# Standing weights stored in alternate words, second activation views moved by 96 bytes

## The chip, the cores and the metric

The kernel runs on one core of one Trainium2 chip, in one launch. The metric is device time in microseconds. Three runs of the kernel before took 1596.76 us in the median (1593.56 to 1600.59).

## The reference, cut to what matters

Two transformer blocks are computed for 256 tokens of width 2048, all in float32. Nearly all of the work is in products of a 256-row activation with a large weight matrix:

```
def first_block(x, c, ...):
    mod = silu(c) @ w_ada + b_ada                  # 2048 x 6144, one row
    h = rms(x) * (1 + scale) + shift
    proj = h @ w_in                                # 2048 x 8192
    ...                                            # chunked attention, gated recurrence
    return x + gate * (concat([att, hg]) @ w_out)  # 2048 x 2048

def second_block(x, mem, ...):
    z = rms(x) @ w_in_2                            # 2048 x 1856
    ...                                            # pooling, latent attention, attention to mem @ w_mem_kv
    x = x + concat([y_pool, y_mla, y_mem]) @ w_o
    h = rms(x)
    return x + (silu(conv3(h @ w_gate)) * (h @ w_up)) @ w_down   # w_gate, w_up: 2048 x 5632
```

## The kernel before

**Products in three parts.** TensorE multiplies in its fast float32 form, which keeps fewer digits. So every weight and every activation stands in SBUF as a high part and a low part, and a product is high times high, high times low activation, and low weight times high activation. Weights come by DMA into the ring `raw` (1 MB each, two halves of 1024 words in each partition). For each half h, ScalarE copies it to the high part (line 1519) and VectorE subtracts to get the low part (line 1916). They go to two tiles, `wh` and `wl`, of four slots each (`WS`), slot h % 4, 4096 bytes a slot. TensorE waits for a half's low part, uses it, and frees the slot with a semaphore.

**Two kinds of halves.** In a *standing* half (function `s`, lines 1169 to 1174) each 128 x 128 block of weights is loaded into the array, and the activations are streamed past it. A block has three matmuls of 256 columns, lines 1169 (high weights, high activations), 1170 (high weights, low activations) and 1171 (low weights, high activations); in the gate and up products of the last stage, the first two are one matmul of 512 columns (line 1173), and the third is line 1174. Every matmul has its own weight load. There are 2736 standing blocks in 342 halves: 512 for `w_in` (reading the view `hA`), 240 for `w_in_2` (`hA2`), 576 for `w_out`, `w_o` and the up-projections (`hB2`), and 1408 for gate and up (`hA2`, the wide ones). In a *moving* half (functions `m`, `chunk`, `memory_row`, `down_part`) it is the other way round: activations are loaded into the array, and 512 columns of weights are streamed. These are lines 1309 to 1311, 1216 to 1218, 1192 to 1194 and 1226 to 1228.

**Where things lie.** In each partition `wh` begins at byte 49280, `wl` at 65664, `hA` at 82048, `hB` at 133248: all at 128 past a multiple of 512. An activation tile of `hA` or `hB` is 2048 bytes: 256 high words, then 256 low words. `hA2` and `hB2` are second views over the same space, 32 bytes further on, used by later stages. A weight block is 512 bytes. The blocks, the parts of an activation and the tiles of each view thus all keep one distance to each other modulo 512: 0 for `hA` and `hB`, 32 for the second views. In the built program the weight load of a block walks its columns from the last to the first (step -1), and the activations are streamed from the first to the last.

**The order of the work** is written by a planner (class `Order`), which keeps TensorE's stream of halves full and puts the small work of attention, recurrence and norms between blocks in six lanes. It plans with its own table of costs, which the change does not touch.

Of the kernel before, what the change touches and what calls it, by code (L numbers as in the profile page):

```python
# [7 lines left out]
F32 = mybir.dt.float32  # L8
# [6 lines left out]
P = 128  # L15
# [11 lines left out]
LANES = 6  # L27

# [187 lines left out]
class Order:  # L216
# [3 lines left out]
    def __init__(self):  # L220
# [32 lines left out]
        self.second = set()  # L253
        self.events = []
# [210 lines left out]
    def m_half(self, tile, banks, kts, buf, first, last):  # L465
        h = self.half
        self.half += 1
        self.want(h + self.ahead)
        self.half_start(h)
        self.beat("m", h, banks, buf, kts, first, last, tile, [self.seen(buf, kt) for kt in kts])  # L470
# [12 lines left out]
    def chunk_half(self, g, n, kt, pair):  # L483
        h = self.half
        self.half += 1
        self.want(h + self.ahead)
        self.half_start(h)
        kts = GROUPS[g][1]
        self.beat("c", h, g, kt, pair, self.seen("A", kt))
        if kt == kts[-1]:  # L490
            for c in (2 * pair, 2 * pair + 1):
                self.beat("part", h, g, c)

    def memory_row(self, kt):
        h = self.half
        self.half += 1
        self.want(h + self.ahead)
        self.half_start(h)
        self.beat("mm", h, kt)

    def down_half(self, kt, pair):
# [3 lines left out]
        self.half_start(h)  # L505
        self.beat("down", h, kt, pair, self.seen("F", kt))
# [3 lines left out]
    def down_end(self, kts):  # L510
# [3 lines left out]
        self.half_start(self.half - 1)  # L514
        self.beat("dend", h, kts)
# [339 lines left out]
def program(nc, table, wts, ada, xN, xT, memN, crow, cst, vec, msk, wpool, dt, out):  # L855
    o = order()
    with ExitStack() as ctx:
# [10 lines left out]
        wh = sb("wh", [P, WS, HALF], F32R)  # L868
        wl = sb("wl", [P, WS, HALF], F32R)
# [3 lines left out]
        at[0] += 32  # L873
# [5 lines left out]
        early = nc.alloc_sbuf_tensor_at("early", [P, 4096], F32, offset=at[0] + 32)  # L879
        E1 = nc.alloc_sbuf_tensor_at("E1", [P, 512], F32, offset=at[0] + 32 + 15 * 2048)[:, :]  # L880
        hB_off = at[0]
        hB = sb("hB", [P, KT, 512], F32R)
        at[0] += 32
# [40 lines left out]
        mark, after = counts.mark, counts.after  # L924

# [188 lines left out]
        def _(e):  # L1114
# [23 lines left out]
            for b in o.beats:  # L1138
                if b[0] == "load" and b[1] >= RAW:
                    load(b[1])  # L1140
                elif b[0] == "consts":
                    e.dma_start(mk[:].rearrange("p a b -> p (a b)"), msk).then_inc(s_mask, 16)
# [12 lines left out]
        def _(e):  # L1155
            def s(h, j, bank, buf, kt, first, last, tile, fresh):
                hl = moving[buf][:, kt % KT, :]
                w1, w2 = wh[:, h % WS, j * P:(j + 1) * P], wl[:, h % WS, j * P:(j + 1) * P]
# [21 lines left out]
            def m(h, banks, buf, kts, first, last, tile, fresh):  # L1180
                e.wait_ge(s_lo, h + 1)
                for j, kt in enumerate(kts):
                    w1, w2 = wh[:, h % WS, j * 512:(j + 1) * 512], wl[:, h % WS, j * 512:(j + 1) * 512]
# [13 lines left out]
            def chunk(h, g, kt, pair, fresh):  # L1197
# [4 lines left out]
                for i in (1, 0) if g == 0 and kt == kts[0] and pair == 0 else (0, 1):  # L1202
                    c = 2 * pair + i
                    w1, w2 = wh[:, h % WS, i * 512:(i + 1) * 512], wl[:, h % WS, i * 512:(i + 1) * 512]
# [16 lines left out]
            def down_part(h, kt, c, t, first, last):  # L1221
                w1, w2 = (w[:, h % WS, c % 2 * 512:c % 2 * 512 + 512] for w in (wh, wl))
# [75 lines left out]
            def memory_row(h, kt):  # L1298
                e.wait_ge(s_lo, h + 1)
                e.wait_ge(*moving_ready("B", kt))  # L1300
                for i in (1, 0) if kt == 0 else (0, 1):
                    if kt == 0 and i == 0:
                        e.wait_ge(*after(("open",), "dve", ("cb", 3)))
                    w1, w2 = wh[:, h % WS, i * 512:(i + 1) * 512], wl[:, h % WS, i * 512:(i + 1) * 512]
# [209 lines left out]
        def _(e):  # L1514
            def split(h, n, part):
# [3 lines left out]
                e.activation(wh[:, h % WS, :], raw[:, n % RAW, part * HALF:(part + 1) * HALF], ACT.Copy).then_inc(s_hi)  # L1519
# [392 lines left out]
        def _(e):  # L1912
            def split(h, n, part):
                src = raw[:, n % RAW, part * HALF:(part + 1) * HALF]
                e.wait_ge(s_hi, h + 1)
                e.tensor_tensor(wl[:, h % WS, :], src, wh[:, h % WS, :].bitcast(F32), ALU.subtract).then_inc(s_lo)  # L1916
# [111 lines left out]
            def rec(t, k):  # L2028
# [3 lines left out]
                def pick(li):  # L2032
# [8 lines left out]
                    if li == 0:  # L2041
                        src = bank[:, :].rearrange("p (a w) -> p a w", a=4)
                        mask = mk[:, 0, :].unsqueeze(1).broadcast_to([P, 4, P])
                    else:
# [4 lines left out]
                        mask = mk[:, li, 0:64].rearrange("p (n w) -> p n w", w=h).unsqueeze(1).broadcast_to([P, 4, n, h])  # L2049
# [481 lines left out]
def constants():  # L2531
# [30 lines left out]
    return c, m.reshape(P, -1)  # L2562
# [65 lines left out]
```

## Time and profile before

| | |
|---|---|
| median of the runs | 1596.76 us |
| the profiled execution, span | 1599.0 us |
| PE busy, matmuls | 1573.0 us (98%), 9650 |
| PEld busy, weight loads | 1400.7 us (88%), 9650 |
| DVE busy | 1154.1 us (72%) |
| ACT busy | 862.4 us (54%) |
| chain that ended last | PE 89%, DVE 5%, DMA 3% |

The page comes from one execution. Its share of busy time says that an engine had some instruction in it, not that it worked at its peak: a matmul of 256 columns is shown as 0.28 us long, while the next one starts 0.12 us after it. What a matmul costs in a dense stream is therefore read from the distance of starts. A weight load (PEld) runs beside the matmul before its own. The granted clock is at its higher level, 2.4 GHz, in nearly every slice.

### The profile page before, as it was taken

To read this page: it belongs to the slowest core of one execution; us is meant where nothing else is said; L and a number is where in the kernel's file an instruction comes from. 1 tells how busy PE (TensorE), PEld (TensorE's weight loads), DVE (VectorE), ACT (ScalarE), POOL (GpSimd) and SP (SyncE) were. 2 spreads that over 40 slices of the span, in tenths; PEclk is the share of its full clock that TensorE was granted. 3 is DMA by queue.
4 is the path that set the end of the run, shared out by engine and by line. 5 is a ranking of instruction groups with operands and counts; after the bars stand their busy time and mean duration, and the time that the engine had idled before them with its cause. 6 is when DMAs were issued, how large, how long until landed. Compare 5 with 4: busy or idle time off the path is not lost.

```text
span 1599.0 us, 24289 instructions
## 1 busy us (share of the span) xinstructions
PE 1573.0 (98%) x9650; PEld 1400.7 (88%) x9650; DVE 1154.1 (72%) x1696; ACT 862.4 (54%) x1321; POOL 151.6 (9%) x164
## 2 busy tenths in 40 slices
PE   8998999989999999999999999999999999999999
PEld 6787889988999999988799888888888888888887
DVE  6797867877778886759778777777777777455544
ACT  6855546767665555655556454544444444444442
POOL 0000000321221220034213000000000000000000
PEclk9999999999999999999999999999999999999999
DMA  9999975533457774343244545555455454555552
GB/s 373 369 343 349 365 285 209 188 114 121 180 189 267 285 272 179 132 158 132 97 144 178 189 170 199 184 186 210 172 197 191 179 211 175 205 199 185 198 196 105
DMA packets 47825, 331.02 MB, mean 207 GB/s; under 512 B 5281, under 2 KB 6689, under 8 KB 8417
## 3 DMA queue, kind: packets, MB, share of 16 engines
q1 hardware_dynamic: 45184, 312.20, 53.5%
q0 software_dynamic: 2240, 17.04, 2.8%
q8 instruction: 76, 1.25, 0.3%
q14 instruction: 35, 0.29, 0.1%
q10 hardware_dynamic: 290, 0.25, 0.1%
HBM read 327.37 MB, written 2.10 MB: 206 GB/s over the span
## 4 chain that ended last, share of the span: by engine, by line
PE 89%; DVE 5%; DMA 3%; ACT 2%; issue 1%; POOL 0%; SPq 0%; ACTq 0%; DVEq 0%; POOLq 0%
PE ps L1173 20%; PE ps L1174 11%; PE ps L1169 9%; PE ps L1170 8%; PE ps L1171 8%; PE ps L1228 5%; PE ps L1227 5%; PE ps L1226 5%; PE ps L1216 4%; PE ps L1217 3%; PE ps L1218 3%; DVE wl L1916 2%; DMA raw<-in_wts 1%; DMA xs<-in_xN 1%; PE ps L1384 1%; PE ps L1351 1%
## 5 line engine op out<-in xcount | busy, mean ns | idle before, releaser
L1916 DVE TENSOR_TENSOR wl<-raw,wh 128x1024 fp32r<-128x1024 f32 x512 | 626.2, 1236 | 282.4 <-ACT wh L1519 281.9
L1519 ACT ACTIVATE wh<-raw 128x1024 fp32r<-128x1024 f32 x512 | 531.3, 1054 | 377.2 <-PE ps L1228 130.6
L1173 PE MATMUL ps<-hA,wh 128*128 128x512 f32 x1408 | 488.7, 390 | 0.0
L1174 PE MATMUL ps<-hA,wl 128*128 128x256 f32 x1408 | 397.0, 282 | 0.0
L1173 PEld LDWEIGHTS ps<-hA,wh 128*128 128x128 f32 x1408 | 264.2, 188 | 55.3
L1174 PEld LDWEIGHTS ps<-hA,wl 128*128 128x128 f32 x1408 | 266.1, 189 | 0.0
L1169 PE MATMUL ps<-hA,wh 128*128 128x256 f32 x752 | 219.5, 292 | 0.0
L1170 PE MATMUL ps<-hA,wh 128*128 128x256 f32 x752 | 211.7, 282 | 0.0
L1171 PE MATMUL ps<-hA,wl 128*128 128x256 f32 x752 | 211.7, 282 | 0.0
L1169 PE MATMUL ps<-hB,wh 128*128 128x256 f32 x576 | 164.4, 285 | 0.8 <-DVE work L2362 0.4
L1170 PE MATMUL ps<-hB,wh 128*128 128x256 f32 x576 | 161.1, 280 | 0.0
L1171 PE MATMUL ps<-hB,wl 128*128 128x256 f32 x576 | 160.6, 279 | 0.0
L1169 PEld LDWEIGHTS ps<-hA,wh 128*128 128x128 f32 x752 | 143.2, 190 | 2.7 <-issue 1.9
L1170 PEld LDWEIGHTS ps<-hA,wh 128*128 128x128 f32 x752 | 143.3, 191 | 0.7 <-issue 0.2
L1171 PEld LDWEIGHTS ps<-hA,wl 128*128 128x128 f32 x752 | 143.1, 190 | 0.0
L1226 PE MATMUL ps<-wh,hB 128*128 128x512 f32 x352 | 137.0, 389 | 0.0
L1227 PE MATMUL ps<-wl,hB 128*128 128x512 f32 x352 | 136.9, 389 | 0.0
L1228 PE MATMUL ps<-wh,hB 128*128 128x512 f32 x352 | 136.9, 389 | 0.0
L1169 PEld LDWEIGHTS ps<-hB,wh 128*128 128x128 f32 x576 | 108.2, 188 | 5.2 <-issue 4.0
L1170 PEld LDWEIGHTS ps<-hB,wh 128*128 128x128 f32 x576 | 108.3, 188 | 0.3 <-issue 0.2
L1171 PEld LDWEIGHTS ps<-hB,wl 128*128 128x128 f32 x576 | 108.3, 188 | 0.0
L1216 PE MATMUL ps<-wh,hA 128*128 128x512 f32 x256 | 101.4, 396 | 4.2 <-ACT xs L1701 3.3
(303 smaller groups left out, 2077.9 us busy)
## 6 DMA issues: line engine op xcount, KB each, us to landing
raw<-in_wts SPq DMA_DIRECT2D x256, 1024.0 KB, 4.8
raw<-in_ada SPq DMA_DIRECT2D x36, 1024.0 KB, 6.1
side<-in_ada POOLq DMA_DIRECT2D x12, 1024.0 KB, 8.5
work<-in_memN SPq DMA_DIRECT2D x2, 1024.0 KB, 8.9
xs<-in_xN POOLq DMA_DIRECT2D x1, 2048.0 KB, 20.6
xs<-in_xT POOLq DMA_DIRECT2D x2, 1024.0 KB, 7.8
out_rows<-xs SPq DMA_DIRECT2D x8, 256.0 KB, 2.4
wp<-in_dt SPq DMA_DIRECT2D x8, 128.0 KB, 2.7
```

Of the source, the lines that this page charges most:

```text
L1169: e.matmul(po, w1, hl[:, 0:T], start=first, stop=False)
L1170: e.matmul(po, w1, hl[:, T:2 * T], start=False, stop=False)
L1171: i = e.matmul(po, w2, hl[:, 0:T], start=False, stop=last)
L1173: e.matmul(ps[bank][:, :], w1, hl, start=first, stop=False)
L1174: i = e.matmul(ps[bank][:, T:2 * T], w2, hl[:, 0:T], start=False, stop=last)
L1216: e.matmul(po, hi, w1, start=kt == kts[0], stop=False)
L1217: e.matmul(po, hi, w2, start=False, stop=False)
L1226: e.matmul(po, hi, w1, start=first, stop=False)
L1227: e.matmul(po, hi, w2, start=False, stop=False)
L1228: return e.matmul(po, lo, w1, start=False, stop=last)
L1519: e.activation(wh[:, h % WS, :], raw[:, n % RAW, part * HALF:(part + 1) * HALF], ACT.Copy).then_inc(s_hi)
L1916: e.tensor_tensor(wl[:, h % WS, :], src, wh[:, h % WS, :].bitcast(F32), ALU.subtract).then_inc(s_lo)
```

## The change

The two tiles `wh` and `wl` become one, `wb`, with four slots of 8192 bytes, in the same space. A new function `weights(h)` says where the parts of half h lie. For a moving half they lie as before, 1024 high words and then 1024 low words (`o.moved` holds these halves). For a standing half they lie column by column in alternate words: high in the even words, low in the odd ones. So ScalarE writes every second word of the slot, VectorE reads one set and writes the other, and a weight load of TensorE walks 128 words in steps of two, over 1024 bytes instead of 512. The activations are still streamed forwards.

The second views `hA2` and `hB2` lie 128 bytes past the first ones (`VIEW`) instead of 32. The mask tile `mk` is packed (576 bytes instead of 1024) to make room for that. The instructions of every engine, their order and their waits are the same; only the addresses and steps of operands differ, and the DMA of the masks is smaller.

```
+VIEW = 128
...
-        wh = sb("wh", [P, WS, HALF], F32R)
-        wl = sb("wl", [P, WS, HALF], F32R)
+        wb = sb("wb", [P, WS, 2 * HALF], F32R)
...
         hA = sb("hA", [P, KT, 512], F32R)
-        at[0] += 32
+        at[0] += VIEW
...
-        early = nc.alloc_sbuf_tensor_at("early", [P, 4096], F32, offset=at[0] + 32)
+        early = nc.alloc_sbuf_tensor_at("early", [P, 4096], F32, offset=at[0] + VIEW)
...
-        mk = sb("mk", [P, len(LEVELS), P], U8, 1)
+        mk = sb("mk", [P, P + 64 * (len(LEVELS) - 1)], U8, 1)
...
-        hA2 = nc.alloc_sbuf_tensor_at("hA2", [P, KT, 512], F32R, offset=hA_off + 32)
-        hB2 = nc.alloc_sbuf_tensor_at("hB2", [P, KT, 512], F32R, offset=hB_off + 32)
+        hA2 = nc.alloc_sbuf_tensor_at("hA2", [P, KT, 512], F32R, offset=hA_off + VIEW)
+        hB2 = nc.alloc_sbuf_tensor_at("hB2", [P, KT, 512], F32R, offset=hB_off + VIEW)
...
+        def weights(h):
+
+            slot = wb[:, h % WS, :]
+            if h in o.moved:
+                return slot[:, 0:HALF], slot[:, HALF:2 * HALF]
+            return slot[:, 0::2], slot[:, 1::2]
...
             def s(h, j, bank, buf, kt, first, last, tile, fresh):
                 hl = moving[buf][:, kt % KT, :]
-                w1, w2 = wh[:, h % WS, j * P:(j + 1) * P], wl[:, h % WS, j * P:(j + 1) * P]
+                w1, w2 = (w[:, j * P:(j + 1) * P] for w in weights(h))
...
-                e.activation(wh[:, h % WS, :], raw[:, n % RAW, part * HALF:(part + 1) * HALF], ACT.Copy).then_inc(s_hi)
+                e.activation(weights(h)[0], raw[:, n % RAW, part * HALF:(part + 1) * HALF], ACT.Copy).then_inc(s_hi)
...
                 e.wait_ge(s_hi, h + 1)
-                e.tensor_tensor(wl[:, h % WS, :], src, wh[:, h % WS, :].bitcast(F32), ALU.subtract).then_inc(s_lo)
+                hi, lo = weights(h)
+                e.tensor_tensor(lo, src, hi.bitcast(F32), ALU.subtract).then_inc(s_lo)
```

## Rows read from the trace of the kernel before

**Rows 1.** Stretches by stage: us busy and count of PE, PEld, DVE, ACT, POOL; clock, DMA.

```profile
0.00:251.00 251.00, 238.11 (x1028) 192.47 (x1029) 191.44 (x205) 144.72 (x206) 7.26 (x17) 0.98 0.90 341
251.00:863.00 612.00, 602.48 (x4711) 572.89 (x4711) 473.90 (x817) 382.15 (x664) 142.06 (x145) 0.99 0.49 177
863.00:1356.00 493.00, 493.00 (x2860) 437.54 (x2859) 368.00 (x553) 236.53 (x338) 2.27 (x2) 1.00 0.52 188
1356.00:1599.00 243.00, 239.46 (x1056) 197.78 (x1055) 120.74 (x125) 98.99 (x114) 0.00 (x0) 1.00 0.51 182
```

**Rows 2.** Timeline of PE in the `w_in` product (view `hA`): start us, length, line.

```profile
420.87 0.28 PE L1171 MATMUL ps<-hA,wl 128*128 128x256 f32 x1
...
422.19 0.28 PE L1170 MATMUL ps<-hA,wh 128*128 128x256 f32 x1
```

**Rows 3.** The same in the `w_in_2` product (view `hA2`, 32 bytes on).

```profile
637.05 0.28 PE L1169 MATMUL ps<-hA,wh 128*128 128x256 f32 x1
...
638.22 0.28 PE L1170 MATMUL ps<-hA,wh 128*128 128x256 f32 x1
```

**Rows 4.** The wide line 1173 in 1000 to 1300 us: shortest/median/longest ns, first and last start.

```profile
L1173 PE MATMUL ps<-hA,wh x866: 390/390/390, 999.8 to 1299.7; 128*128 128x512 f32 x174
```

**Rows 5.** Timeline of PE in that stage.

```profile
1101.04 0.39 PE L1173 MATMUL ps<-hA,wh 128*128 128x512 f32 x1
1101.27 0.28 PE L1174 MATMUL ps<-hA,wl 128*128 128x256 f32 x1
1101.38 0.39 PE L1173 MATMUL ps<-hA,wh 128*128 128x512 f32 x1
```

**Rows 6.** Line 1226, moving weights, one of three equal matmuls, 1400 to 1590 us.

```profile
L1226 PE MATMUL ps<-wh,hB x280: 389/389/472, 1400.0 to 1589.9; 128*128 128x512 f32 x140
```

**Rows 7.** The chain of waits: start, us, what. Transposes of 128 columns, each with a load.

```profile
886.92 1.75 PE ps L1263 x16
```

**Rows 8.** Timeline of PE: float32 matmuls in two passes each, 256 columns.

```profile
635.84 0.59 PE L1395 MATMUL ps<-work 128*128 128x256 f32 x2
636.27 0.59 PE L1399 MATMUL ps<-work 128*128 128x256 f32 x2
```

**Rows 9.** VectorE, 256 columns from SBUF: lines 2067 (steps of two and more) and 2308 (dense).

```profile
L2067 DVE TENSOR_TENSOR work<-E,work x6: 407/416/465, 350.5 to 487.5; 128x256 f32<-128x256 f32 x6
L2308 DVE TENSOR_TENSOR work<-ps,work x88: 416/422/426, 870.8 to 1357.1; 128x256 f32<-128x256 f32 x88
```

**Rows 10.** The page's costliest groups: busy us, mean ns, idle before and its releaser.

```profile
L1916 DVE TENSOR_TENSOR wl<-raw,wh 128x1024 fp32r<-128x1024 f32 x512 | 626.2, 1236 | 282.4 <-ACT wh L1519 281.9
L1519 ACT ACTIVATE wh<-raw 128x1024 fp32r<-128x1024 f32 x512 | 531.3, 1054 | 377.2 <-PE ps L1228 130.6
```

**Rows 11.** Stretches of the mixed stages, columns as in Rows 1.

```profile
300.00:350.00 50.00, 45.53 (x338) 43.07 (x337) 38.33 (x85) 32.68 (x64) 14.01 (x14) 0.93 0.36 128
350.00:400.00 50.00, 46.85 (x358) 44.23 (x357) 40.47 (x94) 38.18 (x80) 13.23 (x15) 0.97 0.35 122
...
550.00:575.00 25.00, 24.61 (x205) 23.85 (x204) 24.86 (x31) 10.91 (x17) 4.55 (x4) 1.00 0.88 335
```

**Rows 12.** The chain of waits in the `w_out` product.

```profile
556.67 2.20 DVE raw L1962
558.87 0.02 DVE cols L1962
...
559.04 1.22 DVE wl L1916
560.26 0.39 DVE xs L2348
560.65 1.13 DVE wl L1916
```

More of the change, by code:

```diff
@@ L253, in __init__ @@
         self.second = set()
+        self.moved = set()
         self.events = []
@@ L498, in memory_row @@
         self.half_start(h)
+        self.moved.add(h)
         self.beat("mm", h, kt)
@@ L505, in down_half @@
         self.half_start(h)
+        self.moved.add(h)
         self.beat("down", h, kt, pair, self.seen("F", kt))
@@ L514, in down_end @@
         self.half_start(self.half - 1)
+        self.moved.update(range(h, h + 2 * len(kts)))
         self.beat("dend", h, kts)
@@ L1182, in m @@
                 for j, kt in enumerate(kts):
-                    w1, w2 = wh[:, h % WS, j * 512:(j + 1) * 512], wl[:, h % WS, j * 512:(j + 1) * 512]
+                    w1, w2 = (w[:, j * 512:(j + 1) * 512] for w in weights(h))
                     if fresh[j]:
@@ L1203, in chunk @@
                     c = 2 * pair + i
-                    w1, w2 = wh[:, h % WS, i * 512:(i + 1) * 512], wl[:, h % WS, i * 512:(i + 1) * 512]
+                    w1, w2 = (w[:, i * 512:(i + 1) * 512] for w in weights(h))
                     if kt == kts[0]:
@@ L1221, in down_part @@
             def down_part(h, kt, c, t, first, last):
-                w1, w2 = (w[:, h % WS, c % 2 * 512:c % 2 * 512 + 512] for w in (wh, wl))
+                w1, w2 = (w[:, c % 2 * 512:c % 2 * 512 + 512] for w in weights(h))
                 hi = hB[:, kt % KT, t * P:(t + 1) * P]
@@ L1303, in memory_row @@
                         e.wait_ge(*after(("open",), "dve", ("cb", 3)))
-                    w1, w2 = wh[:, h % WS, i * 512:(i + 1) * 512], wl[:, h % WS, i * 512:(i + 1) * 512]
+                    w1, w2 = (w[:, i * 512:(i + 1) * 512] for w in weights(h))
                     for t in range(2):
@@ L2042, in pick @@
                         src = bank[:, :].rearrange("p (a w) -> p a w", a=4)
-                        mask = mk[:, 0, :].unsqueeze(1).broadcast_to([P, 4, P])
+                        mask = mk[:, 0:P].unsqueeze(1).broadcast_to([P, 4, P])
                     else:
@@ L2048, in pick @@
                         src = bank[:, 0:T].rearrange("p (a n w) -> p a n w", a=4, w=h)
-                        mask = mk[:, li, 0:64].rearrange("p (n w) -> p n w", w=h).unsqueeze(1).broadcast_to([P, 4, n, h])
+                        mask = mk[:, P + 64 * (li - 1):P + 64 * li].rearrange("p (n w) -> p n w", w=h).unsqueeze(1).broadcast_to([P, 4, n, h])
                     e.copy_predicated(dst, mask, src).then_inc(mark(t, "dve", ("p", li)))
@@ L2561, in constants @@
             m[:, n, 0:64] = (s // (2 * h) == late // (2 * h)) & (s % (2 * h) < h)
-    return c, m.reshape(P, -1)
+    return c, np.concatenate([m[:, 0]] + [m[:, n, 0:64] for n in range(1, len(LEVELS))], 1)
 def kernel(**inputs):
```

8 lines of the change are left out of this document (5 added, 3 removed).

## The prediction

> **What bounds the kernel now.** I read the stages first [rows 1]. From 251 to 1356 us, where all standing halves lie, TensorE is busy nearly throughout: 602 of 612 us, then 493 of 493. In the wide stage VectorE has 368 us of work in 493 and ScalarE 237, so both follow TensorE. What a block costs on TensorE is what that stage costs. So the question is how far apart its matmuls start, and why.
>
> In the `w_in` product eleven steps take 422.19 - 420.87 = 1.32 us: 120.0 ns for a matmul of 256 columns [rows 2]. At the granted 2.4 GHz 256 columns are 106.7 ns; 13.3 ns are on top. The same matmuls over the view that lies 32 bytes further take 1.17 us for ten steps, 117 ns [rows 3]. The instructions are alike, the distance of the addresses is not: part of the surcharge hangs on where weights and activations lie to each other. In the wide stage a block takes 299.9 / 865 = 346.7 ns [rows 4], about 230 and 115 [rows 5]; 768 columns are 320, so 26.7 ns are on top, 13.3 for each matmul again. With moving weights it is (189.9 / 279) / 3 = 226.9 ns, against 213.3 for 512 columns [rows 6]: again 13.5.
>
> Two kinds of rows have nearly no surcharge. Sixteen transposes of 128 columns, each with its load, take 1.75 us, 109.4 ns each [rows 7]. A stream of 128 columns would be 53 ns, so this is the load of 128 weight columns: 106.7 ns at one column per cycle of 1.2 GHz, and 2.7. And float32 matmuls of 256 columns in two passes start 0.43 / 2 = 215 ns apart [rows 8]: there a pass takes in one column per cycle of 1.2 GHz (213.3 ns), just as the load beside it, and only some 2 ns are on top. In the fast form the stream takes eight bytes in that time and the load four, and 13 ns are on top.
>
> **The change part by part.** The reading of these rows on which I build: a load and a stream that read SBUF at the same time now and then want the same piece of it, and one of them is held up; how often depends on their distance and on their relative pace. This is inferred, no row shows a held-up read.
>
> *Loads of standing weights in steps of two words.* They now pass eight bytes for each column, as many as the stream does in the same time. The nearest rows with equal pace have 2 to 3 ns on top [rows 7, 8]. That is the good end: 109.4 ns for a matmul of 256 columns (it can't go below the load) and 213.3 + 2.1 + 109.4 = 324.8 for a wide block. The other end is that the load fetches pieces of fixed size, twice as many as before, and each has the same price: 13.3 ns more for each load. I take 112 ns for 256 columns and 331 for a wide block, nearer to the first end, since the equal pace is the property that both cheap rows share; I do not take the end itself, since in them a stream at half rate has time to catch up, and here it has none.
>
> The count: `w_in` has 512 blocks or 1536 matmuls, 1536 x (120 - 112) = 12.3 us. The other narrow ones are 816 blocks or 2448 matmuls, 2448 x (117 - 112) = 12.2 us. The wide ones are 1408 x (346.7 - 331) = 22.1 us. Together 46.6 us of TensorE. At the good end: 1536 x 10.6 + 2448 x 7.6 + 1408 x 21.9 = 16.3 + 18.6 + 30.8 = 65.7 us.
>
> *What of it reaches the end.* The wide stage: all, since VectorE's 368 us and ScalarE's 237 fit into 493 - 22 = 471 [rows 1]. In the `w_in` stage TensorE already waits at 300 to 400 us (busy 92.4 of 100) with the other engines at 71 to 79 us [rows 11]; its recurrence hangs on VectorE, ScalarE and GpSimd. I keep half of the 12.3 us. In the `w_out` product VectorE is busy for 24.86 of 25 us [rows 11], and the chain of waits runs through it alone [rows 12]: conversions, sums and the 2.2 us products for the gate's modulation. There, some 30 us long, a faster TensorE brings nothing, 30 x 4% = 1.3 us; with the attention tails I take 3 us off the 12.2. So 6.1 + 9.2 + 22.1 = 37 us are left.
>
> *The conversions write and read every second word.* There are 342 such halves, 1.24 us each on VectorE and 1.05 on ScalarE [rows 10]. VectorE operations of 256 columns in steps of two and more take 416 ns, dense ones 422 [rows 9]: the step costs nothing, and I take zero. No row shows ScalarE writing in steps. Its bounds are zero and one more such instruction, 1.05 us for each half; over the 176 wide halves that is 185 us on top of 237, still under 471, so the price would be lateness at a half's start, which three halves of lead hide. If VectorE did pay its 1.24 us twice, it would need 368 + 218 = 586 us in that stage and be the bound; [rows 9] speaks against it, and I leave it in the slow cases.
>
> *Moving halves.* High and low part are now 4096 bytes apart, not 16384; modulo 512 nothing changes, and the first views lie as before. I take 0; at 1 ns either way for each of 2040 matmuls it would be 2 us.
>
> *The second views 128 bytes on.* A shift of 32 bytes was worth 3 ns of 120 [rows 2, 3]. With equal pace and both walks in opposite directions the distance decides where they meet, so the shift may be worth anything between the ends above. It is in the 112. The 24 matmuls that load from `hB2` (lines 1192 to 1194) are too few to count. The packed mask saves 57 KB of one DMA that nobody waits for.
>
> **The Trainium skill.** The rows show that the surcharge moves with the address, 120.0 against 117 ns [rows 2, 3]. The Trainium skill, "TensorE: Matmul & The Clock Gate", Part 2, says that TensorE has two independent SBUF read ports, so that loading the next weights takes nothing from the running matmul; by this rule the change would do nothing, the third rival below. The rows speak against the rule's strict form. The Trainium skill, "SBUF — State Buffer", Specifications, says that lines are 16 bytes and that two hits on each are needed for the full rate; steps of two float32 words give just two. No row here has a load in steps; if it failed, that is the second rival.
>
> **The rivals.** (1) *Twice the pieces, twice the stalls*: slower. Each standing load today carries up to 13.3 ns and would carry 13.3 more. There are 3984 narrow and 2816 wide loads: 6800 x 13.3 = 90 us, 1687 us. It decides once a load's surcharge goes above today's 10 to 13 ns. For it: in all dense fast-form rows the surcharge goes with the load, whether the stream has 256 or 512 columns [rows 2, 5, 6], as if each load had a fixed number of pieces. Against it: the same load beside a float32 stream costs 2 ns [rows 8]. (2) *A load in steps of two runs at half rate*: 109.4 x 2 = 219 ns. The narrow matmuls would cost 219 instead of 118, 3984 x 101 = 402 us, and the narrow half of a wide block 219 instead of 115, 146 us: about 2145 us. (3) *The surcharge is not reading but the exchange of weights in the array*: no change, 1597 us. For it: that it is 13.3 in three places; against it: [rows 3, 7]. (4) *Only one kind of view gains*: where the distance is unlucky the stream still meets the load as often as before. With the first views alone, 6 us: 1591; this is hardly to be told from no change.
>
> **How the numbers follow.** Profiled: 1599.0 - 37 = 1562; the median of the runs is 2.2 us lower, so 1560. Chances: the forecast, both kinds of view gaining, 0.55; rival 1 in any size 0.21; rival 2 or a VectorE that pays for steps 0.04; rival 3 0.10; rival 4 0.10, half of which lies beyond 0.5%. About 0.5%, 8 us, is what a measurement can tell from no change. So faster 0.60, same 0.15, slower 0.25. The range runs from the good end, 1597 - 66 = 1531, over no change, to 1612, where a mild form of rival 1 (2 ns for each load) still lies; the strong forms stay outside.
>
> **What would show it.** Right: in the profile of the changed kernel, steps of about 112 ns at lines 1169 to 1171 and 331 ns for a wide block, VectorE's line for the low part still at about 1.24 us, ScalarE's at 1.05. Wrong: steps of 130 ns or more (rival 1), 219 (rival 2), 120 and 347 (rival 3), or second views that stay at 117 and 347 while `hA` falls (rival 4). If TensorE's steps fall and the time does not, look at 300 to 400 and 540 to 575 us for VectorE.

## The result, and the profile after

The changed kernel takes 1620.26 us in the median of four runs (1617.19 to 1621.64). The kernel before, run beside it, takes 1597.72 us (1593.56 to 1600.59). The ratio is 1.0137 (95% interval 1.0117 to 1.0157): 22 us slower. The profiled execution has a span of 1615.4 us against 1599.0.

The first view is the page of the changed kernel: totals, then its costliest groups (line, operation, shapes, count | us busy, mean ns of one | idle before and its releaser).

```profile
PE 1591.8 (99%) x9650; PEld 1418.6 (88%) x9650; DVE 1155.4 (72%) x1696; ACT 894.5 (55%) x1321; POOL 151.2 (9%) x164
...
L1930 DVE TENSOR_TENSOR wb<-raw,wb 128x1024 fp32r<-128x1024 f32 x512 | 626.0, 1236 | 295.3 <-ACT wb L1532 294.5
L1532 ACT ACTIVATE wb<-raw 128x1024 fp32r<-128x1024 f32 x512 | 564.3, 1121 | 373.0 <-PE ps L1241 130.5
L1186 PE MATMUL ps<-hA,wb 128*128 128x512 f32 x1408 | 501.1, 401 | 0.0
L1187 PE MATMUL ps<-hA,wb 128*128 128x256 f32 x1408 | 394.7, 280 | 0.0
L1186 PEld LDWEIGHTS ps<-hA,wb 128*128 128x128 f32 x1408 | 277.8, 197 | 56.5
```

The lines have moved: 1169 to 1171 are now 1182 to 1184, 1173 and 1174 are 1186 and 1187, 1226 is 1239, 1519 is 1532, 1916 is 1930. VectorE's low parts cost what they did, 1236 ns a half [rows 10]. ScalarE's high parts went from 1054 to 1121 ns in the mean. That mean mixes moving and standing halves. If the 67 ns belong to the 342 standing halves of 512, each of these takes 67 x 512 / 342 = 100 ns more. Half by half the trace shows just that: 342 copies went from 1053 to 1152 ns in the mean, the other 170 stayed within 2 ns. Columns here: shortest/median/longest ns, first and last start.

```profile
L1532 ACT ACTIVATE wb<-raw x512: 1039/1140/1215, 11.3 to 1600.9; 128x1024 fp32r<-128x1024 f32 x171
```

Next, stretches by stage, with the columns of [rows 1] (busy us and count of PE, PEld, DVE, ACT, POOL; clock, DMA).

```profile
251.00:863.00 612.00, 603.62 (x4659) 575.11 (x4659) 468.66 (x808) 394.74 (x658) 140.15 (x143) 0.99 0.49 176
863.00:1356.00 493.00, 493.00 (x2799) 438.21 (x2798) 359.78 (x539) 248.03 (x334) 3.81 (x4) 1.00 0.51 184
```

In both kernels TensorE fills the stretch from 863 to 1356 us, at the same clock of 1.00. Before, it got 2860 matmuls in [rows 1]; now it gets 2799. At about 178 ns each, these 61 are 11 us. From 251 to 863 us it is 52 fewer (4711 before), at about 120 ns 6 us. So the loss lies where standing weights are used, and it is a price per matmul: TensorE is never idle longer in the wide stage, it is busy all along and gets less done.

The wide line of the changed kernel, from 1000 to 1300 us, answers to [rows 4], and the timeline of TensorE in that stage (start us, length us, line) to [rows 5]:

```profile
L1186 PE MATMUL ps<-hA,wb x845: 398/401/403, 999.9 to 1300.0; 128*128 128x512 f32 x169
L1186 PEld LDWEIGHTS ps<-hA,wb x844: 197/197/198, 1000.1 to 1299.9; 128*128 128x128 f32 x169
```

```profile
1101.10 0.28 PE L1187 MATMUL ps<-hA,wb 128*128 128x256 f32 x1
1101.22 0.40 PE L1186 MATMUL ps<-hA,wb 128*128 128x512 f32 x1
1101.45 0.28 PE L1187 MATMUL ps<-hA,wb 128*128 128x256 f32 x1
1101.57 0.40 PE L1186 MATMUL ps<-hA,wb 128*128 128x512 f32 x1
```

A wide block takes (1300.0 - 999.9) / 844 = 355.6 ns, against 346.7. It is all in the matmul of 512 columns: in the mean 238.9 ns to the next start instead of 228.3, while the 256 columns behind it take 116.7 instead of 118.3. Over 1408 blocks, 8.9 ns are 12.5 us.

The narrow matmuls over the first view did not change: here the `w_in` product again, sixteen starts of which the first and the last are shown, (422.58 - 420.78) / 15 = 120.0 ns as in [rows 2].

```profile
420.78 0.28 PE L1182 MATMUL ps<-hA,wb 128*128 128x256 f32 x1
...
422.58 0.28 PE L1182 MATMUL ps<-hA,wb 128*128 128x256 f32 x1
```

Those over the second view `hB2` did. First the kernel before, then the changed one, in the same stretch of their `hB2` products; 40 starts lie between the first and last row of the former, 39 in the latter:

```profile
839.76 0.28 PE L1169 MATMUL ps<-hB,wh 128*128 128x256 f32 x1
...
844.59 0.28 PE L1171 MATMUL ps<-hB,wl 128*128 128x256 f32 x1
```

```profile
839.76 0.28 PE L1183 MATMUL ps<-hB,wb 128*128 128x256 f32 x1
...
844.61 0.29 PE L1184 MATMUL ps<-hB,wb 128*128 128x256 f32 x1
```

That is 4.83 / 41 = 117.8 ns before and 4.85 / 40 = 121.2 after. The mean over all narrow matmuls of the second views rose by as much, from 117.1 to 120.7. Over these 2448, 3.5 ns are 8.6 us. With the wide blocks it makes 21 us of the measured 22.

The two profiled executions show where this arrives: the first line of the narrow blocks over `hA` and `hA2`, before and after, then the wide line, before and after.

```profile
L1169 PE MATMUL ps<-hA,wh x752: 277/283/679, 252.0 to 723.3; 128*128 128x256 f32 x188
L1182 PE MATMUL ps<-hA,wb x752: 278/283/681, 249.0 to 724.1; 128*128 128x256 f32 x188
L1173 PE MATMUL ps<-hA,wh x1408: 390/390/581, 863.8 to 1355.5; 128*128 128x512 f32 x176
L1186 PE MATMUL ps<-hA,wb x1408: 392/401/580, 867.6 to 1371.8; 128*128 128x512 f32 x176
```

The wide stage lasts 491.7 us before and 504.2 after: its 12.5 us arrive in full. From the first narrow start to the first wide one it is 611.8 and 618.6 us: 6.8 of the 8.6 arrive. Together that is 19 us. The spans differ by 16.4, since the first standing half began 3.0 us earlier in this execution of the changed kernel; executions of one kernel lie up to some 10 us apart, and what made this one earlier stays open.

The rest of this study asks which of the two parts of the change did it, and why.

### The profile page after: what moved, and what is told of

The parts are those of the page before. It is cut to its first block, busy times and chain, and to the rows that moved or that the text cites. A ratio compares the mean times of both kernels' runs of the same rounds, so it can differ in the third digit from the quotient of the medians.

```text
span 1615.4 us, 24289 instructions
## 1 busy us (share of the span) xinstructions
PE 1591.8 (99%) x9650; PEld 1418.6 (88%) x9650; DVE 1155.4 (72%) x1696; ACT 894.5 (55%) x1321; POOL 151.2 (9%) x164
## 4 chain that ended last, share of the span: by engine, by line
PE 87%; DVE 5%; DMA 3%; ACT 3%; issue 1%; POOL 0%; SPq 0%; ACTq 0%; DVEq 0%; POOLq 0%
PE ps L1186 21%; PE ps L1187 10%; PE ps L1182 10%; PE ps L1183 9%; PE ps L1184 9%; PE ps L1239 5%; PE ps L1240 5%; PE ps L1241 5%; PE ps L1229 2%; PE ps L1231 2%; PE ps L1230 2%; DMA raw<-in_wts 2%; DVE wb L1930 2%; PE ps L1397 1%; DMA xs<-in_xN 1%
## 5 line engine op out<-in xcount | busy, mean ns | idle before, releaser
L1930 DVE TENSOR_TENSOR wb<-raw,wb 128x1024 fp32r<-128x1024 f32 x512 | 626.0, 1236 | 295.3 <-ACT wb L1532 294.5
L1532 ACT ACTIVATE wb<-raw 128x1024 fp32r<-128x1024 f32 x512 | 564.3, 1121 | 373.0 <-PE ps L1241 130.5
L1186 PE MATMUL ps<-hA,wb 128*128 128x512 f32 x1408 | 501.1, 401 | 0.0
L1187 PE MATMUL ps<-hA,wb 128*128 128x256 f32 x1408 | 394.7, 280 | 0.0
L1186 PEld LDWEIGHTS ps<-hA,wb 128*128 128x128 f32 x1408 | 277.8, 197 | 56.5
L1187 PEld LDWEIGHTS ps<-hA,wb 128*128 128x128 f32 x1408 | 277.8, 197 | 0.0
L1182 PE MATMUL ps<-hA,wb 128*128 128x256 f32 x752 | 220.7, 293 | 0.0
L1183 PE MATMUL ps<-hA,wb 128*128 128x256 f32 x752 | 212.7, 283 | 0.0
L1184 PE MATMUL ps<-hA,wb 128*128 128x256 f32 x752 | 212.6, 283 | 0.0
L1182 PE MATMUL ps<-hB,wb 128*128 128x256 f32 x576 | 166.2, 288 | 0.5 <-DVE work L2376 0.5
L1183 PE MATMUL ps<-hB,wb 128*128 128x256 f32 x576 | 163.5, 284 | 0.0
L1184 PE MATMUL ps<-hB,wb 128*128 128x256 f32 x576 | 163.3, 283 | 0.0
L1182 PEld LDWEIGHTS ps<-hA,wb 128*128 128x128 f32 x752 | 146.7, 195 | 2.7 <-issue 1.9
L1183 PEld LDWEIGHTS ps<-hA,wb 128*128 128x128 f32 x752 | 146.8, 195 | 0.6 <-issue 0.2
L1184 PEld LDWEIGHTS ps<-hA,wb 128*128 128x128 f32 x752 | 146.7, 195 | 0.0
L1239 PE MATMUL ps<-wb,hB 128*128 128x512 f32 x352 | 137.0, 389 | 0.0
L1240 PE MATMUL ps<-wb,hB 128*128 128x512 f32 x352 | 136.9, 389 | 0.0
L1241 PE MATMUL ps<-wb,hB 128*128 128x512 f32 x352 | 136.9, 389 | 0.0
L1182 PEld LDWEIGHTS ps<-hB,wb 128*128 128x128 f32 x576 | 112.3, 195 | 4.3 <-issue 4.1
L1184 PEld LDWEIGHTS ps<-hB,wb 128*128 128x128 f32 x576 | 112.4, 195 | 0.0
L1183 PEld LDWEIGHTS ps<-hB,wb 128*128 128x128 f32 x576 | 112.1, 195 | 0.3 <-issue 0.2
L1229 PE MATMUL ps<-wb,hA 128*128 128x512 f32 x256 | 101.1, 395 | 4.0 <-ACT xs L1714 3.0
```

What stands on the lines that cost most here:

```text
L1182: e.matmul(po, w1, hl[:, 0:T], start=first, stop=False)
L1183: e.matmul(po, w1, hl[:, T:2 * T], start=False, stop=False)
L1184: i = e.matmul(po, w2, hl[:, 0:T], start=False, stop=last)
L1186: e.matmul(ps[bank][:, :], w1, hl, start=first, stop=False)
L1187: i = e.matmul(ps[bank][:, T:2 * T], w2, hl[:, 0:T], start=False, stop=last)
L1229: e.matmul(po, hi, w1, start=kt == kts[0], stop=False)
```

## The experiments

### One part of the change at a time

The first kernel has the second views 128 bytes on, but all weights in dense halves.

```
-            if h in o.moved:
-                return slot[:, 0:HALF], slot[:, HALF:2 * HALF]
-            return slot[:, 0::2], slot[:, 1::2]
+            return slot[:, 0:HALF], slot[:, HALF:2 * HALF]
```

> The changed kernel with the layout undone: high and low parts of standing halves in two runs of 1024 words again, second views still 128 bytes on. Theory L (the layout costs, the distance is innocent): the wide block falls back to 346.7 ns or below and the second views' narrow matmuls to 117, the time to 1597 us or a little less. Theory D (the distance of 128 costs by itself): wide block 355 ns, narrow 120.5, about 1620 us less what ScalarE gives back (its copy for standing halves from 1.15 to 1.05 us). Theory P (the two together cost, since pace and distance only matter in company): somewhere else, and the run with alternate words at 32 bytes tells. In all, the w_in stage stays at 120.0 ns.

Measured: 1609.18 us, ratio 1.0072 (1.0048 to 1.0097), 11 us slower than before. Its wide line in the same stretch:

```profile
L1184 PEld LDWEIGHTS ps<-hA,wb x855: 187/188/188, 999.8 to 1299.7; 128*128 128x128 f32 x171
L1184 PE MATMUL ps<-hA,wb x855: 387/396/398, 999.9 to 1299.8; 128*128 128x512 f32 x171
```

A block takes 299.9 / 854 = 351.2 ns, and the narrow matmuls over second views start 119.1 ns apart in the mean. Loads are back at 188 ns and ScalarE's copies at 1054. So moving the views alone costs half of the loss, and the steps account for it: 1408 x 4.5 = 6.3 and 2448 x 2.0 = 4.9 us.

The second kernel has the alternate words, with the views at the old 32 bytes.

```
-VIEW = 128
+VIEW = 32
```

> The changed kernel with the distance undone: alternate words kept, second views 32 bytes on. Theory L (layout costs): narrow matmuls of the second views at 120 to 121 ns, wide block about 355, 1615 to 1625 us. Theory D (distance costs): narrow 117, wide 346.7, about 1598 us. Theory P: neither. ScalarE's copy stays at about 1.12 us in the mean in every theory.

Measured: 1617.32 us, ratio 1.0122 (1.0099 to 1.0145), 19 us slower.

```profile
L1186 PE MATMUL ps<-hA,wb x850: 398/398/398, 999.7 to 1299.7; 128*128 128x512 f32 x170
L1186 PEld LDWEIGHTS ps<-hA,wb x850: 197/197/197, 1000.0 to 1300.0; 128*128 128x128 f32 x170
```

Here a wide block takes 300.0 / 849 = 353.4 ns, and `hB2` matmuls 120.7 (the mean over both second views is 120.65, 3.5 more than before). By steps that is 1408 x 6.7 = 9.4 and 2448 x 3.5 = 8.6, 18 of the 19 us. So both parts cost, 11 and 19 us, and together they cost 22 and not 31: neither is a fixed price for each load. Each combination of layout and distance has a step of its own.

### A table of steps without the other engines

The next kernel leaves the whole computation out. TensorE runs twenty blocks for each layout and distance and nothing else runs beside it. *Narrow* is the kernel's triple of 256 columns, *wide* its pair of 512 and 256.

```
def narrow(layout, v):
    for i in range(20):
        ...
        w1, w2 = weight(layout, h, j, 0), weight(layout, h, j, 1)
        hi, lo = stream(layout, i % 16, v, 0, T), stream(layout, i % 16, v, T, T)
        yield o, w1, hi, True, False
        yield o, w1, lo, False, False
        yield o, w2, hi, False, True
```

> A kernel that leaves the whole computation out and only measures: 77 patterns of weight loads and matmuls on TensorE, 20 blocks each, no other engine at work. Narrow blocks (three matmuls of 256 columns) and wide blocks (512 and 256), with weights dense or in alternate words, activations streamed forwards or backwards, and the activations 0 to 384 bytes past the grid of the weights. Three patterns with steps of 3, 4 and 8 words, two with three matmuls of 64 columns for each set of weights. If reads of one place collide: dense and forwards 120.0 ns at 0 and 117 at 32, 346.7 for a wide block at 32, and other numbers at other distances; with alternate words and backwards both walks keep one distance, so the surcharge is either nearly gone (110 to 112 ns, 326 to 330 for a wide block) or large, by the distance alone. If the surcharge is the exchange of weights: 120 in every pattern, which the 117 of the kernel before already speaks against. Steps of 3, 4 and 8 words tell what a load that leaves a 16-byte piece after one or two words costs: 110 to 120 ns if nothing, 219 or more if it is paid for.

Here are three lines of its trace: dense at distance 32, alternate at 128, and the wide blocks alternate at 128. The starts are printed to 0.1 us; the table below is worked out from starts in ns, without the first two blocks of each.

```profile
L90 PE MATMUL ps<-hs,wb x60: 277/279/282, 51.6 to 58.5; 128*128 128x256 f32 x60
...
L111 PE MATMUL ps<-hs,wb x60: 281/283/288, 199.9 to 207.1; 128*128 128x256 f32 x60
...
L120 PE MATMUL ps<-hs,wb x40: 280/339/403, 264.1 to 271.1; 128*128 128x512 f32 x20, 128*128 128x256 f32 x20
```

| distance, bytes | 0 | 16 | 32 | 64 | 96 | 128 | 192 | 256 |
|---|---|---|---|---|---|---|---|---|
| narrow, dense, ns a matmul | 120.0 | 118.7 | 116.7 | 113.3 | 120.0 | 118.7 | 113.3 | 119.9 |
| narrow, alternate | 120.0 | 118.3 | 120.0 | 120.1 | 120.0 | 121.1 | 120.0 | 120.0 |
| wide, dense, ns a block | 353.5 | 346.7 | 346.9 | 352.9 | 350.1 | 351.0 | 353.4 | 353.5 |
| wide, alternate | 353.5 | 353.2 | 353.2 | 353.3 | 351.2 | 355.3 | 351.2 | 346.7 |

This shows three things. The kernels' steps are here without any other engine: alternate at 128, 121.1 and 355.3 (120.7 in the mean and 355.6 in the changed kernel); dense at 128, 118.7 and 351.0 (119.1 and 351.2); alternate at 32, 120.0 and 353.2 (120.65 and 353.4). So VectorE's and ScalarE's strided accesses are not needed for them; within 1 ns a matmul they have no part in it. Second, alternate words are better by more than 1 ns only for wide blocks at 192 and 256 bytes, and at 256 the next table has 346.7 for dense weights too; narrow ones lie at 120 where dense ones reach 113.3 and 116.7. Third, the change took the worst column for its own layout.

The same kernel streams the activations backwards, so that load and stream walk the same way. Narrow matmuls take 117.8 to 120.0 ns (dense) and 117.8 to 123.6 (alternate). Wide blocks take 351.1 to 353.5 and 351.0 to 360.0. Direction is no cure either. And it loads weights in steps of three and four words (lines 160 and 161):

```profile
L160 PEld LDWEIGHTS ps<-hs,wb x60: 252/262/266, 547.8 to 558.1; 128*128 128x128 f32 x60
L160 PE MATMUL ps<-hs,wb x60: 332/338/349, 547.9 to 558.2; 128*128 128x256 f32 x60
L161 PEld LDWEIGHTS ps<-hs,wb x60: 321/330/334, 558.3 to 572.1; 128*128 128x128 f32 x60
L161 PE MATMUL ps<-hs,wb x60: 393/395/399, 558.4 to 572.2; 128*128 128x256 f32 x60
```

10.3 / 59 = 175 ns a matmul for steps of three words, 13.8 / 59 = 234 for steps of four: the load is then the limit, as with steps of eight words (241.7). Steps of two words keep the load's rate (195 ns in the record against 188). This is what the Trainium skill, "SBUF — State Buffer", Specifications, states: two hits on each 16-byte line are needed for full rate. The trace agrees, 120, 175 and 234 ns for steps of two, three and four.

The last patterns of this kernel are matmuls of 64 columns, each with a dense load, at distance 0. While the granted clock is 1.00 (to 589 us), they start 111.6 ns apart, 5 above the 106.7 at which the prediction puts the load, though their stream walks as fast as that of the longer ones. Then, after 40 us of loads in steps of three to eight words with TensorE busy throughout, the clock falls to 0.50, and the same matmuls take 213 ns.

### Does the table hold in the kernel?

If the steps belong to distances, a better distance must make the kernel faster. First `hB2` at 64 bytes, all weights dense, `hA2` at 32 as before the change.

```
+VIEW_A = 32
+VIEW_B = 64
...
+        hB2 = nc.alloc_sbuf_tensor_at("hB2", [P, KT, 512], F32R, offset=hB_off + VIEW_B)
```

> High and low parts in runs again as in the kernel before, hA2 back at 32 bytes, hB2 at 64 instead of 32. Theory G (the surcharge is a property of one load beside one stream and their distance, and the pattern kernel m1_grid gives it): the 1728 matmuls over hB2 fall from 117.4 to 113.3 ns, 7.1 us on TensorE, of which some 1.5 us are lost where VectorE is the bound, so about 1592 us; the wide block stays at 346.7. Rival: in the kernel, with ScalarE, VectorE and DMA writing SBUF at the same time, the pattern's numbers don't hold and the time stays at 1597 to 1598.

A miss: 1598.86 us against 1599.73, ratio 0.9998 (0.9984 to 1.0012). The `hB2` matmuls took 117.6 ns, and not 113.3. The run shows one thing besides: it has the merged tile `wb` and the packed mask, and the time of the kernel before, so these parts of the change cost nothing.

So I measured the table more finely, again with the computation left out, and asked what the surcharge needs: a stream that walks, or a load that walks?

> The whole computation is left out again; patterns on TensorE alone. Narrow and wide blocks, dense weights, forwards, at distances from 0 to 448 bytes in finer steps; blocks of moving weights (three matmuls of 512, the load 0 to 384 bytes past the grid of the stream); and patterns in which the stream, the load or both read one and the same word all the time (narrow for the first three, 512 columns for the last two). If the surcharge comes from two reads that want the same piece of SBUF, a stream or a load that stays on one word must change it: with the load on one word 107 to 112 ns for 256 columns and 214 to 218 for 512, with both likewise. If a part of it is the exchange of weights or a fixed cost of a matmul, that part stays: 113 ns, the lowest value seen so far, or 120. Moving weights: 226.7 at 0 and 232 at 32, as in the kernel; at 64 not known.

| distance, bytes | 0 | 32 | 48 | 64 | 96 | 112 | 128 | 160 | 192 | 224 | 256 |
|---|---|---|---|---|---|---|---|---|---|---|---|
| narrow, dense | 120.0 | 116.7 | 118.4 | 117.8 | 119.9 | 113.3 | 118.7 | 117.3 | 113.3 | 118.3 | 119.9 |
| wide, dense | 346.7 | 346.9 | 351.1 | 353.2 | 350.3 | 353.4 | 350.7 | 346.7 | 353.4 | 346.7 | 346.7 |

At 64 bytes it is 117.8 this time, and was 113.3 the first. Wide blocks at 0 are 346.7 here and 353.5 there. Some distances have two steps and keep to one of them for the whole run of 20 blocks. Narrow matmuls at 112 and 192 gave 113.3 in both tables as far as they have them. For moving weights, 512 columns, it is 226.8 at 0, 226.7 at 16, 240 and 256 bytes, 228.9 at 192, and 232 to 234 from 32 to 160; the kernel before has 226.9 at 0 [rows 6].

The next two lines are matmuls of 256 columns whose *stream* stays on one word while the load walks (172), and whose *load* stays on one word while the stream walks (174), both at distance 0; then moving weights at 0 and 64 bytes.

```profile
L172 PE MATMUL ps<-hs,wb x60: 272/275/275, 493.0 to 499.6; 128*128 128x256 f32 x60
...
L174 PE MATMUL ps<-hs,wb x60: 282/283/283, 506.4 to 513.5; 128*128 128x256 f32 x60
...
L154 PE MATMUL ps<-wb,hs x42: 389/389/398, 318.1 to 327.4; 128*128 128x512 f32 x42
...
L158 PE MATMUL ps<-wb,hs x42: 392/393/398, 356.7 to 366.3; 128*128 128x512 f32 x42
```

With the stream on one word a matmul takes 6.6 / 59 = 112 ns (111.67 from the finer starts). With the load on one word it is 120.0 at distance 0 and 116.65 at distance 32, just as when the load walks. So of the 13.3 ns, 5 are there even when the stream does not walk, and up to 8.3 come with a walking stream; the walk of the load is not needed for them. With 512 columns it is alike: 217.8 ns with the stream on one word, 4.4 above 213.3, and 231.7 (distance 0) and 231.1 (32) with the load on one word. These rows give no ground for a plan to remove the surcharge through the load's pace.

Then the distance that was steady, 192 bytes, for `hB2` alone (`VIEW_B = 192`), and for `hA` as well: `hA` begins 192 bytes past the grid of weights, `hA2` 32 past it.

> As e3_hB64, but hB2 at 192 bytes. In both pattern kernels 192 gave 113.33 ns (at 64 one gave 113.33 and the other 117.78, so what stood before decides there). If 192 holds its low step in the kernel too: 1728 matmuls over hB2 at 113.3 to 114 instead of 117.4, up to 7 us on TensorE, 1592 to 1594 us. If the kernel's breaks (waits, small matmuls of the lanes) put the pair into the other step there as well: 117 to 119 ns, 1597 to 1600 us.

Measured: 1596.20 us against 1599.38, ratio 0.9981 (0.9968 to 0.9994). The `hB2` matmuls are at 114.9 ns in the mean, a mixture of starts 113 to 114 and 117 to 118 ns apart: the low step is held only part of the time. By the mean it is 1728 x 2.4 = 4 us, where up to 7 were expected; 3 were measured.

```
+        grid = at[0]
+        at[0] += SHIFT          # 192
         hA_off = at[0]
...
+        hA2 = nc.alloc_sbuf_tensor_at("hA2", [P, KT, 512], F32R, offset=grid + VIEW_A)
+        hB2 = nc.alloc_sbuf_tensor_at("hB2", [P, KT, 512], F32R, offset=hB_off + VIEW_B)
```

> As e4_hB192, and hA itself at 192 bytes past the grid of the weights (hA2 stays at 32, the constants vs move behind hB). The 1536 narrow matmuls of the w_in product: 113.3 to 114 ns instead of 120, 9 to 10 us on TensorE, half of it lost to the recurrence's own chain. The price: 768 matmuls with moving weights load from hA, 229 instead of 226.7 ns by m2_grid, 1.8 us. Together with hB2 some 7 to 12 us, 1586 to 1591 us; if the step is not held, 1600 us or more.

Measured: 1592.45 us against 1599.38, ratio 0.9958 (0.9942 to 0.9974): the best version of this study, 7 us faster than the kernel before. The timeline of its `w_in` product, with 42 starts between the two rows:

```profile
259.76 0.28 PE L1184 MATMUL ps<-hA,wb 128*128 128x256 f32 x1
...
264.63 0.28 PE L1185 MATMUL ps<-hA,wb 128*128 128x256 f32 x1
```

4.87 / 43 = 113.3 ns, where the kernel before has 120.0 [rows 2]. Over all `w_in` matmuls the mean is 113.8, where it was 119.8: 1536 x 6.1 = 9.3 us of TensorE, and another 1728 x 2.9 = 5 us from `hB2`. Against it stand the moving halves that load from `hA`, at 229 ns and not 227: 768 x 2 = 1.5 us. Of the remaining 13 us, 7 reach the end. The runs with `hB2` alone (e4) and with both (e5) differ by the place of `hA`. From the first standing start to the first over `hB2` it is 254.3 us in the one (251.3 to 505.6) and 248.8 in the other (252.5 to 501.3): 5.5 of the 9.3 us of `w_in` arrive in that stretch, somewhat more than the half that the prediction kept. The medians of these two runs differ by 3.7 us, with some 3 us of uncertainty.

### Why are the slow float32 matmuls cheap?

The prediction rested on [rows 8]: float32 matmuls in two passes have only 2 ns on top. The next kernel, again without the computation, gives them loads in steps of one to four words. It also lets the fast form's stream cycle over a piece of 4 to 128 words.

> The whole computation is left out; patterns on TensorE alone, narrow blocks. (1) The stream walks over the same 4, 8, 16, 32, 64 or 128 words again and again instead of 256 in a row, beside a walking load. m2_grid: on one word 111.7 ns, on 256 words 120.0 and 116.7. The size at which the surcharge comes back is the size of the pieces in which the stream reads. (2) Slow form (float32 in two passes, stream of 256) with the load dense and in steps of 2, 3 and 4 words. The reading on which the prediction built (equal pace is cheap) says: 215 dense, 220 or more with steps of 2, since then the load runs twice as fast as the stream. The rival reading (a slow stream makes up for it whatever the pace): 215 to 217 in both, and 233 with steps of 4, where the load is the bound. (3) The same distance after different patterns, and blocks at 0, 32, 64, 112 and 192 three times as long: does a distance have one step or two? (4) Weights and activations shifted together by 16, 32, 64 and 192: if the distance alone decides, 120.0 in all.

Two-pass float32 (16 passes of 256 columns), loads in steps of two (168), three (170) and four words (172):

```profile
L168 PEld LDWEIGHTS ps<-hf,wf x16: 195/197/197, 135.2 to 138.5; 128*128 128x128 f32 x16
...
L170 PEld LDWEIGHTS ps<-hf,wf x16: 251/252/253, 142.1 to 145.4; 128*128 128x128 f32 x16
...
L172 PEld LDWEIGHTS ps<-hf,wf x16: 309/329/329, 149.1 to 152.5; 128*128 128x128 f32 x16
```

A pass takes 215.9 ns with dense loads, 215.8 with steps of two, 215.8 with steps of three, and 233.3 only with steps of four. If equal pace of load and stream made them cheap, steps of two, which give the load twice the bytes for each column, should have brought the surcharge back; steps of three, whose load lasts 252 ns in the record, surely. They did not. What fits all four figures is that a pass of 213 ns has slack that covers the load until the load itself needs 233; these rows say nothing about pace.

The fast form's stream over a piece of 8 and of 16 words:

```profile
L156 PE MATMUL ps<-hs,wb x60: 275/275/275, 57.5 to 64.1; 128*128 128x256 f32 x60
...
L158 PE MATMUL ps<-hs,wb x60: 286/287/288, 71.0 to 78.2; 128*128 128x256 f32 x60
```

Over 4 and 8 words it is 111.7 ns at distances 0 and 32. Over 16 words it is 123.3 and 120.1, over 32 words 117.8 and 123.4, and from 64 words on 119.9 at 0, as with the full stream, and 117.8 at 32. The part that depends on distance comes back between 32 and 64 bytes of stream. The history was tried as well. Narrow matmuls at 64 bytes took 113.3 ns behind a run at 32 and behind one at 48, and 117.8 behind wide blocks; but the second table had 117.8 behind a run at 48, and in a run of 60 blocks, behind 60 at 32, it is 117.8 again. At 192 it was 113.3 each time but once, 117.8 behind a run at 64. At 32 the 60 blocks take 117.8, where shorter runs took 116.7. So these distances have two steps, and the distance of the run just before does not alone decide which. Weights and activations shifted together by 32, 64 or 192 bytes stay at 120.0, but shifted by 16 bytes they take 118.3, where 120.0 was expected: the distance counts most, and the place is not without effect.

### Does ScalarE's slower copy reach the end?

Steps of TensorE account for 21 of 22 us in the changed kernel and 18 of 19 with alternate words at 32 bytes (e2). Whether ScalarE's slower copies add to that, two kernels can tell that differ in the layout alone, at a distance where the first table has the same steps for both. The last pair puts all second views at distance 0, with alternate words and with dense halves.

```
-VIEW = 128
+VIEW = 0
```

> The changed kernel with its second views at no distance from the first (VIEW = 0); standing weights in alternate words as in the changed kernel. In the table of steps measured without other engines, a distance of 0 gave both layouts the same steps: 120.0 ns for a narrow matmul, and for a wide block 353.5 ns once and 346.7 ns another time. Theory A (the layout costs only through the distances, nothing of it comes from ScalarE's slower copy): this kernel and its dense twin agree within 2 us. Theory B (ScalarE's copies, some 85 ns more for each half, reach the end in the mixed stages): this kernel is 3 to 10 us slower than its dense twin at the same TensorE steps. Against the kernel before: 2448 x 3 = 7.3 us for the narrow matmuls, and 0 or 1408 x 6.8 = 9.6 us for the wide blocks, so 1605 or 1615, plus what theory B adds.

> The dense twin: weights in two dense halves, second views at distance 0. Narrow matmuls at 120.0 ns, wide blocks at 346.7 or 353.5 ns, ScalarE's copies at 1.05 us as in the kernel before. By both theories 1597.7 + 7.3 = 1605 us with wide blocks at 346.7, or 1615 with 353.5. Theory A: the same time as the twin with alternate words within 2 us if the wide blocks take the same step in both. Theory B: 3 to 10 us below it.

Measured: alternate 1608.75 us, ratio 1.0060 (1.0037 to 1.0084); dense 1605.94 us, ratio 1.0035 (1.0022 to 1.0049). The wide lines, alternate first:

```profile
L1186 PE MATMUL ps<-hA,wb x858: 393/394/395, 999.9 to 1299.9; 128*128 128x512 f32 x172
```

```profile
L1184 PE MATMUL ps<-hA,wb x867: 392/392/395, 999.7 to 1299.9; 128*128 128x512 f32 x174
```

A block takes 300.0 / 857 = 350.1 ns with alternate words and 300.2 / 866 = 346.7 with dense halves. The table had 353.5 for the former, and 346.7 or 353.5 for the latter: at 0 a wide block has more than one step. 1408 x 3.4 = 4.8 us for the wide blocks, with narrow ones at 120 in both, is already more than the measured 2.8. Nothing is left for ScalarE, whose copies are 1118 ns here and 1054 in the twin. The two ratios leave some 4 us of uncertainty; theory B's 3 to 10 us beside the 4.8 would have made 8 to 15 us between the twins, where 2.8 were measured. The stages in the two traces say it more sharply. From the first standing start to the first wide one, where theory B places its loss, it is 616.8 us with alternate words (250.5 to 867.3) and 616.6 with dense halves (252.2 to 868.8), though the 166 copies for the standing halves of that stretch take some 100 ns longer. The wide stage lasts 496.6 and 492.1 us, and the 4.5 between them are the wide steps. So the layout costs through TensorE's steps (theory A), as far as one execution of each can tell. The dense twin's 5.6 us over the kernel before are its narrow steps, 2448 x 2.7 = 6.6 us by the means.

## Why the prediction was wrong

**What bounds the kernel**: right. TensorE is the bound in the wide stage in all kernels, and 21 of the 22 us can be counted as steps between its starts. The surcharge in a wide block was read as 13.3 ns for each matmul; by finer starts it is 15.0 for the 512 columns and 11.6 for the 256, which changes nothing in the sum. Reading what a matmul costs there was sound, and so was the remark that part of the surcharge hangs on the distance.

**The failed step** is the reading of [rows 7, 8]: "the equal pace is the property that both cheap rows share". It was the reason for taking 112 and 331 ns. By the prediction's own figures the first row is no case of equal pace at all: its stream of 128 columns needs 53 ns beside a load of 107. What the two rows share is slack: in them the stream is either much shorter than the load or twice as slow, so that a delay of one can be hidden by the other. The runs bear this out. Fast-form matmuls of 64 columns start 111.6 ns apart at distance 0, where 256 columns take 120.0, with the same load and the same pace. Two-pass matmuls stay at 215.8 ns with loads at twice and three times the step, so pace does not make them cheap; and the fast form with a load that stands on one word still takes 120.0 and 116.65. The right comparison would have been a row in which only the pace differs, and no such row was there. I said so for the end of the range, but let the centre go nearly as far.

**The size of what came**: standing matmuls were to fall to 112 and 331 ns. At distance 0 they stayed at 120.0 (0 of the 12.3 us); the narrow ones over second views rose by 3.5 ns (8.6 us, where 12.2 were to be gained), and the wide blocks by 8.9 ns (12.5 us, where 22.1 were to be gained).

**The range** allowed for a mild form of the first rival, 2 ns for each load. The mean of what came over the 6800 standing loads is 21 / 6800 = 3.1 ns, but nothing for the 1536 of `w_in` and 8.9 for the two loads of a wide block. The rival named the right sign by a wrong mechanism: it wanted twice the stalls for twice the pieces, which the unchanged 120.0 at distance 0 refutes. The third rival (the surcharge is an exchange of weights in the array) is refuted for the whole, but has room in about 5 of the 13.3 ns, which are there with a stream on one word; no run shows that they are an exchange of weights. The second rival and a VectorE that pays for steps are refuted by narrow steps of 121 ns, where 219 were to come, and by 1236 ns a half.

**The distance was treated as part of the layout's gain.** "It is in the 112" put the second edit in without a price of its own. [rows 2, 3] had shown that 32 bytes were worth 3 ns of 120; moving the views away from that distance puts those 3 ns at risk whatever else happens. As a term of its own this would have been 0 to 7 us of loss on the narrow matmuls, with an unknown for the wide blocks. Measured alone, it is 11 us.

**The rule weighed there.** The distance alone moves the dense narrow step between 113.3 and 120.0 ns with nothing else running. The Trainium skill, "TensorE: Matmul & The Clock Gate", Part 2, speaks of two independent read ports, so that loading weights takes nothing from the running matmul. By it both parts of the change would have cost nothing on TensorE; the runs show 11 and 19 us. Still open is why the part that depends on distance remains when the load reads a single word, and what the two sides wait for; no run shows a held-up read.

**ScalarE's alternate writes** were taken at zero, with a bound of one more instruction. They cost some 100 ns a standing half, and lie off the path: the last pair's mixed stages are equal within 0.2 us. VectorE, the moving halves (steps of 226.8 ns still) and the packed mask came out as predicted.

## What to carry to other kernels

Where a stream of matmuls is dense, the distance of weights and activations in a partition is a quantity to be set and measured, like a tile size. A table of steps by distance, run by itself on one engine, gave the steps of the whole kernels within about 1 ns a matmul, except at distances with two steps, while an argued mechanism had the wrong sign. When a row looks cheap, ask first whether a slower neighbour hides its cost, before a property of it is credited. And an edit that moves away from an address that was measured as good needs its own term in the sum, even when it is meant to serve another edit.

## What the runs showed of the hardware that I had not expected

- The step of fast-form float32 matmuls with a load each takes a few values that depend on the distance of the addresses: 113.3 to 120.0 ns for 256 columns with dense loads, up to 121.1 with loads in steps of two words and 123.6 with the stream backwards; 226.7 to 234.3 ns for 512 columns of moving weights.
- Some distances have two steps: 113.3 or 117.8 at 64 bytes, 346.7 or 353.5 for wide blocks at 0. The distance of the run just before does not alone decide which one holds. In the changed kernel the `hB2` matmuls run at 120.0 in some stretches and at 121.1 in others.
- A stream that stays within 32 bytes takes 111.7 ns at both distances tried, one over 64 bytes 120.1 and 123.3; a load that stays on one word keeps the surcharge (120.0 and 116.65).
- Loads in steps of two words are nearly free (195 against 188 ns), in steps of three and four they are the limit, 175 and 234 ns a matmul.
- ScalarE writes 1024 words a partition in steps of two some 100 ns slower; VectorE reading and writing so costs nothing (1236 ns in both).
